# Expert gate and up products of a two-layer mixture-of-experts trunk with the weights stationary

## The chip, the cores and the metric

One core of one Trainium2 chip runs the whole program. The metric is the device time of one execution in microseconds (us); the kernel before takes 1674.31 us (median of 3 runs, 1674.31 to 1674.5). Everything is float32.

## What is computed

Two layers of a trunk over 768 tokens (512 latent tokens, 256 context tokens) of width 1024. A layer is: RMSNorm with a modulation computed from a condition vector, one input projection to 2400 columns, four kinds of attention, an output projection, a gated residual; then RMSNorm with modulation, a routed mixture of experts, a gated residual. The second layer needs the latent tokens only. The part that the change is named after:

```
def swiglu(x, wg, wu, wd):
    return (silu(x @ wg) * (x @ wu)) @ wd

out = swiglu(xs, ws_gate, ws_up, ws_down)              # shared expert, hidden width 256
for e in range(16):                                    # 16 experts, hidden width 256
    out = out + gates[:, e:e+1] * swiglu(xs, w_gate[e], w_up[e], w_down[e])
```

`gates` is zero but for two experts of each token: sigmoid scores of a router, the best of four groups of experts, the best two in it, weights normalised to sum 1. The output is the latent stream after a final RMSNorm.

## The kernel before

The order of work is written out by hand, engine by engine: five instruction lists (TensorE `pe`, VectorE `dve`, ScalarE `act`, GpSimd `pool`, SyncE `sp`) that meet at semaphores. SyncE issues nearly all loads and stores, in the order of its list; GpSimd issues the gathers and scatters.

**Start (layer 0).** SyncE loads the condition vectors and the identity (L577 to 580), four 2 MB pieces of the modulation weights (`mod_load`, L595), the bias and gain rows (`mod_rows`, L585, 588), two token tiles, panel 0 of the input projection, four more token tiles; then it waits for the first modulation product and loads panel 1, tables, small weights, and piece 4 of the modulation weights (L649 to 653). TensorE multiplies pieces 0 to 3 (`mod_product`, L1124); VectorE adds the bias rows (`mod_row`, L1830). TensorE turns each normalised token tile (L1142), ScalarE and VectorE write it modulated to `hT` (L885, L1820), and `unit` (L1211) multiplies it by the panel. ScalarE squares tile u+2 before it evacuates tile u+1; the semaphore of tiles 2 to 5 is one, for all four loads. Product 4 stands in the middle of unit 3, product 5 in the middle of unit 5, and so on.

**Experts.** Tokens are sorted by expert into blocks of 128 rows, each block of one expert. The program runs a fixed part and a loop over pairs of blocks whose number comes from the routing. In a block (`e_block`) TensorE does: gate product of block n (`e_in`, L1533), two transposes of block n-1's hidden rows (`hid_turn`, L1385), eight transposes of block n+1's tokens (`e_turn`, L1470), down product of block n-1 (`e_down`, L1543), up product of block n (`e_in` again). The gate and up products have the 128 tokens as the stationary side and the 256 columns of the weights as the moving side:

```
mm = pe.matmul((S0, S1)[b][:, 512 * w:512 * w + DE], XT[b][:, k, :], wgu[b][:, w, k * DE:(k + 1) * DE],
               start=k == 0, stop=k == KT - 1)
```

The result has tokens in its rows, so `hid` must be turned, and VectorE copies it to `hidT` (`e_hid_copy`, L2154) before the down product. VectorE also computes the sigmoid's sum, reciprocal and products (L2130 to L2149) and scales the output into `yb` (`e_out`, L2402). GpSimd scatters `yb` to `y_d` in memory at each token's two rows (L1733), and gathers the tokens of later blocks (L1721). SyncE loads 3 MB of weights a block (L773, L778).

**Seam and end.** The last two blocks of a layer (2 * pairs_2 + 2 and + 3) go partly another way: for the tiles below `late_tiles` (2 in layer 0, 4 in layer 1), `late_rows` (L1589) puts their rows in place by a matmul with a 0/1 matrix, and `c_late` (L2484) adds the result from PSUM. For the other tiles of layer 0 they are scattered (`late_scatter`, L1754). SyncE waits for the scatters, reads `y_d` by tile (L847), and VectorE adds (`y_add` L2442, `c_tile` L2473, L2474). In layer 1, GpSimd does both additions of tile 3 (L1776) and then the rstd steps of all four tiles (L1784, L1786), ScalarE squares (L1109), VectorE scales (`c_final`, L2491), SyncE stores (L857). At the seam SyncE also loads panel 1 of layer 1 (`win_load(1, 1)`), before it waits for the scatters.

**Routing of layer 1.** VectorE's list interleaves routing steps with the shared expert's. `route_places_hot` (L2283) writes the 0/1 matrix from which `route_table` (L1449) makes, by 8 matmuls, the table of tokens by block; `s_down` (L1434) is the shared expert's down product. GpSimd then copies an index (L1718) and gathers.

## Time and profile before

| | |
|---|---|
| Median of 3 runs | 1674.31 us |
| The profiled execution | 1669.1 us |
| its span, from first to last instruction | 1667.2 us |
| TensorE matmuls busy (PE) | 94% of the span |
| VectorE / ScalarE / GpSimd busy | 51% / 26% / 12% |
| TensorE in the chain that ended last | 84% |
| DMA moved | 284.77 MB, mean 171 GB/s |
| Mean granted TensorE clock | 0.987 of full speed |

PE is TensorE's matmuls, PEld its loads of the stationary side, which run beside them. Busy shares are means over stages with different limits; the chain of waits says which work ended last at each moment. In the rows below "issue" is time in which an engine waited for nothing that the profile shows, and a name such as SPq or DVEq is the sequencer of that engine.

### The profile page before, as it was taken

What the parts mean: (1) busy time and instruction counts of PE and PEld (TensorE: products, weight loads), DVE (VectorE), ACT (ScalarE), POOL (GpSimd) and SP (SyncE); (2) the same over time, 40 slices, a digit from 0 to 9 for tenths busy, and PEclk for the clock granted to TensorE, in tenths of its full rate; (3) what the DMA queues carried; (4) which work ended last, traced back from release to release, by engine and by line L of the source; (5) the groups of instructions that cost most, each with busy time, mean ns of one, the idle gap of its engine ahead of it and who ended that gap; (6) DMA issues with size and microseconds to landing.
All of it is one profiled execution on the core that took longest, in us unless ns stands there. A gap on an engine that the chain in (4) does not pass through costs nothing.

```text
span 1667.2 us, 24264 instructions
## 1 busy us (share of the span) xinstructions
PE 1574.3 (94%) x8994; PEld 1024.0 (61%) x8994; DVE 851.4 (51%) x1820; ACT 428.3 (26%) x922; POOL 200.6 (12%) x352
## 2 busy tenths in 40 slices
PE   3999999899999999999999799999899999999997
PEld 3655445666665567777777455555566666677774
DVE  1322433567666566455545621433667665644445
ACT  1312113455454410000000222113455541000001
POOL 0110202000000000212121110202000000022212
PEclk8999999999999999999999899999999999999999
DMA  9674321500001387589897673332401016478884
GB/s 337 197 279 150 104 31 20 190 1 35 18 26 39 105 300 283 171 330 335 326 336 275 228 261 116 137 82 36 174 1 39 14 51 230 181 262 307 321 319 185
DMA packets 107902, 284.77 MB, mean 171 GB/s; under 512 B 32544, under 2 KB 42206, under 8 KB 93406
## 3 DMA queue, kind: packets, MB, share of 16 engines
q1 hardware_dynamic: 97150, 262.48, 45.0%
q0 software_dynamic: 10656, 20.99, 3.4%
q8 instruction: 63, 1.03, 0.3%
q14 instruction: 33, 0.27, 0.1%
HBM read 265.47 MB, written 39.84 MB: 183 GB/s over the span
## 4 chain that ended last, share of the span: by engine, by line
PE 84%; DMA 5%; DVE 3%; SPq 3%; issue 2%; ACT 1%; POOL 0%; POOLq 0%; DVEq 0%; ACTq 0%
PE S L1211 16%; PE S L1533 13%; PE S L1279 9%; PE B L1344 7%; PE S L1543 6%; PE B L1327 6%; PE PT L1296 5%; PE B L1230 3%; PE B L1124 2%; DMA arena<-in_moe_w_up 2%; PE PT L1470 2%; PE S L1230 2%; PE PT L1434 1%; PE S L1410 1%; PE S L1417 1%
## 5 line engine op out<-in xcount | busy, mean ns | idle before, releaser
L1211 PE MATMUL S<-arena 128*128 128x512 f32 (+3 forms) x768 | 298.6, 539 | 6.4 <-issue 4.2
L1533 PE MATMUL S<-arena 128*128 128x256 f32 x1152 | 258.3, 381 | 4.7 <-DMA arena<-in_moe_w_up 3.6
L1533 PEld LDWEIGHTS S<-arena 128*128 128x128 f32 x1152 | 219.2, 191 | 51.5 <-issue 23.5
L1211 PEld LDWEIGHTS S<-arena 128*128 128x128 f32 x768 | 141.2, 192 | 127.7 <-issue 109.3
L989 ACT ACTIVATE arena<-S,nmax 128x768 f32<-128x768 f32 (+1 forms) x200 | 161.8, 812 | 164.6 <-DVE nmax L2016 123.2
L2016 DVE TENSOR_REDUCE nmax<-S 128x1 f32<-128x768 f32 (+1 forms) x168 | 133.1, 825 | 77.8 <-PE S L1279 77.5
L1279 PE MATMUL S<-arena 64*128 64x256 f32 (+5 forms) x720 | 161.7, 499 | 5.8 <-ACT arena L989 4.0
L1344 PE MATMUL B<-arena 128*128 128x512 f32 x320 | 156.5, 613 | 1.9 <-DVE arena L2070 1.9
L1296 PEld LDWEIGHTS PT<-cst,arena 128*128 128x128 f32 x832 | 94.6, 141 | 84.1 <-issue 56.9
L1296 PE MATMUL PT<-cst,arena 128*128 128x128 f32 x832 | 121.2, 278 | 18.8 <-issue 11.3
L1543 PE MATMUL S<-arena 128*128 128x512 f32 x288 | 130.1, 594 | 1.2 <-DVE arena L2154 1.2
L1279 PEld LDWEIGHTS S<-arena 64*128 64x128 f32 (+2 forms) x720 | 75.1, 187 | 68.2 <-issue 59.0
L1008 ACT ACTIVATE arena<-PT 128x768 f32<-128x768 f32 (+3 forms) x100 | 81.1, 811 | 118.5 <-PE PT L1299 59.5
L1327 PE MATMUL B<-arena 128*64 128x128 f32 x1664 | 108.5, 277 | 2.5 <-issue 2.4
L1327 PEld LDWEIGHTS B<-arena 128*64 128x64 f32 x1664 | 89.4, 137 | 22.5 <-issue 22.5
L1041 ACT ACTIVATE arena<-S 128x256 f32<-128x256 f32 x36 | 13.8, 383 | 346.0 <-PE S L1533 346.0
L1344 PEld LDWEIGHTS B<-arena 128*128 128x128 f32 x320 | 54.4, 189 | 53.1 <-issue 48.8
L1543 PEld LDWEIGHTS S<-arena 128*128 128x128 f32 x288 | 52.4, 192 | 55.0 <-issue 55.0
L2131 DVE RECIPROCAL arena<-arena 128x256 f32<-128x256 f32 x46 | 80.6, 1753 | 1.6
L1124 PE MATMUL B<-arena,cs 128*32 128x128 f32 x1536 | 51.3, 291 | 28.7 <-DMA arena<-in_w_mod 17.1
L1830 DVE TENSOR_TENSOR arena<-B,arena 128x128 f32<-128x128 f32 x24 | 6.9, 290 | 137.0 <-PE B L1124 112.1
L2154 DVE COPY arena<-B 128x256 f32<-128x256 f32 x36 | 15.3, 424 | 114.0 <-PE B L1385 114.0
(306 smaller groups left out, 1789.1 us busy)
## 6 DMA issues: line engine op xcount, KB each, us to landing
arena<-in_w_mod SPq DMA_DIRECT2D x24, 2048.0 KB, 10.6
arena<-in_moe_w_gate SPq DMA_DIRECT2D x36, 1024.0 KB, 6.0
arena<-in_moe_w_up SPq DMA_DIRECT2D x36, 1024.0 KB, 8.9
arena<-in_moe_w_down SPq DMA_DIRECT2D x36, 1024.0 KB, 6.0
arena<-in_w_in SPq DMA_DIRECT2D x6, 2048.0 KB, 11.4
arena<-y SPq DMA_DIRECT2D x20, 512.0 KB, 7.0
arena<-mod SPq DMA_DIRECT2D x16, 512.0 KB, 15.9
arena<-in_tokens SPq DMA_DIRECT2D x12, 512.0 KB, 9.5
```

Of the source, the lines that this page charges most:

```text
L989: act.activation(p_buffer(k, m)[:, 0:nk], (S0, S1)[m][:, 0:nk], ACT.Exp, bias=nmax[:, 2 * k + m:2 * k + m + 1], accum_out=rsum[:, 2 * k + ...
L1008: act.activation(t_buffer(k, 1)[:, 0:width], PT[:, 0:width], ACT.Copy).then_inc(s["pt_s"], 1)
L1124: mm = pe.matmul(bank[32 * q:32 * q + 32, 0:MODQ], cs[:, k, :], mod_w[l][n][:, k, q * MODQ:(q + 1) * MODQ], start=k == 0, stop=k == KT - 1)
L1211: mm = pe.matmul(ubank[u % 4][:, c0:PANEL_W[p]], hT[:, k, t * P:(t + 1) * P], panel[p][:, k, c0:], start=k == 0, stop=k == KT - 1)
L1230: mm = pe.matmul(nb_bank(n)[:, 0:c1 - c0], panel[4][:, k, w0:w0 + P], hT[:, k, c0:c1], start=k == 0, stop=k == KT - 1)
L1279: mm = pe.matmul((S0, S1)[m][:, c0:c1], qk[rows, qs, cols], qk[rows, ks, NTOK - nk + c0:NTOK - nk + c1], start=True, stop=True)
L1296: tr = pe.transpose(PT[:, c0:c0 + P], p_buffer(k, m)[:, c0:c0 + P], ident)
L1327: mm = pe.matmul(B6[64 * m:64 * m + 64, 0:P], vals[:, (NTOK - nk) // P + j, v0 + 64 * m:v0 + 64 * m + 64], bufs[m][:, j * P:j * P + P], st ...
L1344: mm = pe.matmul(B7[:, :], OT[t % 2][:, j, :], wout[:, j, c * 512:(c + 1) * 512], start=at_ == 0, stop=at_ == KT - 1)
L1533: mm = pe.matmul((S0, S1)[b][:, 512 * w:512 * w + DE], XT[b][:, k, :], wgu[b][:, w, k * DE:(k + 1) * DE], start=k == 0, stop=k == KT - 1)
L1543: mm = pe.matmul((S0, S1)[b][:, c * 512:(c + 1) * 512], hidT[b][:, k, :], wdn[b][:, k, c * 512:(c + 1) * 512], start=k == 0, stop=k == 1)
L2016: dve.tensor_reduce(nmax[:, 2 * k + m:2 * k + m + 1], Sm[:, 0:nk], AX.X, ALU.max, negate=True).then_inc(s["neg_max"], 1)
```

## The change

- Gate and up products: the weights are the stationary side (two pieces of 128 of the 256 hidden columns), the 128 turned tokens the moving side. The result has hidden columns in its rows. The turn, its copy and `hidT`'s use in experts go; the down product reads `hid`, and `down_load` arranges the weights' rows as (k p) instead of (p k).
- First loads: the condition vectors, the identity and layer 0's bias and gain rows are issued by ScalarE. SyncE issues piece 4 of the modulation weights before panel 1. VectorE normalises tile 0 after the modulation rows and tile 1 after tile 0's evacuation.
- Seam: `win_load(1, 1)` is issued after the reads of tiles 0 and 1. `c_tile` is split in `c_first` and `c_second`, and VectorE evacuates tile t before the first.
- Layer 1: `route_places_hot` before the last up multiplication; `route_table` before the last turn of hidden rows; the first gathers take their index from `token_of` directly; the first down loads wait for gather 0.
- End of layer 1: rows of tiles 2 and 3 in block 2 * pairs_2 + 2 are scattered, and their reads wait for that; `late_rows` of those tiles is left only for the last block. `c_late(2)` and `c_late(3)` move forward by one step.

```diff
         for n in range(4):
             mod_load(0, n, 0)
-        sp.wait_ge(zeros_set, 2)
-        mod_rows(0, 0, NMCH, (0, 1))
         for t in range(2):
             x_load(t)
         win_load(0, 0)
         for t in range(2, T):
             x_load(t)
-        sp.wait_ge(s["mod_mm"], 1)
+        mod_load(0, 4, 2)
         win_load(0, 1)
         sp.dma_start(cst[:, first:], cst_d[:, first:]).then_inc(tables_in, 16)
         gain_load(0)
         small_load(0)
-        mod_load(0, 4, 2)
         sp.wait_ge(zeros_set, 3)
         for layer in range(DEPTH):
             sp.dma_start(relpad[1:61, layer * P + 48:layer * P + 79], A["na_rel_bias"][layer].rearrange("h a b -> (h a) b")).then_inc(rel_step, 16)
...
     def down_load(b, e):
-        src = A["moe_w_down"][l].rearrange("e (p k) n -> e p (k n)", k=2)[bass.ds(e, 1)].rearrange("o p n -> (o p) n")
-        sp.dma_start(wdn[b].rearrange("p a b -> p (a b)"), src).then_inc(s[f"e_dn_in{b}"], 16)
+        src = A["moe_w_down"][l].rearrange("e (k p) n -> e p k n", k=2)[bass.ds(e, 1)].rearrange("o p k n -> (o p) k n")
+        sp.dma_start(wdn[b], src).then_inc(s[f"e_dn_in{b}"], 16)
     def expert_of(blk):
...
         in_load(0, 0, e0)
         in_load(1, 1, e1)
-        sp.wait_ge(s["e_idx"], ge(0) + 2)
+        sp.wait_ge(e_x_in[l][0], 16)
         down_load(0, e0)
         down_load(1, e1)
         sp.dma_start(fgain, A["final_norm"].partition_broadcast(P)).then_inc(s["c_x_in"], 16)
...
         for b in range(2):
             w_load(2 * i + 2 + b, b)
-    if l == 0:
-        win_load(1, 1)
     for b in range(2):
         sp.wait_ge(e_stored[l][b], 16 * (pairs_1 + 1))
...
     for t in range(nt):
         if t == late_tiles[l]:
+            if l == 0:
+                win_load(1, 1)
             for b in range(2):
                 sp.wait_ge(e_stored[l][b], 16 * (pairs_1 + 2))
                 sp.sem_inc(s["spare_seen"], 1)
+        if l and t == LATE_FIRST:
+            sp.wait_ge(e_stored[l][0], 16 * (pairs_1 + 2))
+            sp.sem_inc(s["spare_seen"], 1)
         if l == 0 and t == T - 1:
             sp.wait_ge(late_y, late_tiles[0])
...
 @block.scalar
 def _(act):
+act.dma_start(csrc[:, 0, :], A["c"].rearrange("a (p k) -> (a p) k", k=KT)).then_inc(cond_in, 16)
+act.dma_start(csrc[:, 1, :], A["c_ctx"].rearrange("(p k) -> p k", k=KT)).then_inc(cond_in, 16)
+first = at["ident"][1]
+act.dma_start(cst[:, 0:first], cst_d[:, 0:first]).then_inc(consts_in, 16)
 act.wait_ge(cond_in, 32)
 act.activation(ctmp[:, :, :], csrc[:, :, :], ACT.Exp, scale=-1.0).then_inc(s["small_exp"], 1)
+act.wait_ge(zeros_set, 2)
+for r in range(2):
+    act.dma_start(mod_row0[r:P:32], A["b_mod"][0].rearrange("(n q c) -> q n c", q=4, c=MODQ)).then_inc(s["mod_rows_in"], 16)
+    for half in range(2):
+        gain = A[("norm_mix", "norm_ffn")[half]][0]
+        act.dma_start(mod_norm_at(0, half)[r:P:32], gain.rearrange("(n q c) -> q n c", q=4, c=MODQ)).then_inc(s["mod_rows_in"], 16)
 for l in range(DEPTH):
     g = lambda t: t + T * l
...
         s_down(1)
         s_turn_hid(2)
         s_up(3)
+        pe.wait_ge(s["r_took"], 2)
+        route_table()
         pe.wait_ge(s["s_hts"], g(2) + 1)
         s_turn_hid(3)
-        pe.wait_ge(s["r_took"], 2)
-        route_table()
         s_down(2)
         s_down(3)
...
     def e_in(blk, b, w):
-        for k in range(KT):
-            mm = pe.matmul((S0, S1)[b][:, 512 * w:512 * w + DE], XT[b][:, k, :], wgu[b][:, w, k * DE:(k + 1) * DE],
-                           start=k == 0, stop=k == KT - 1)
+        for h in range(2):
+            to = (S0, S1)[b][:, 512 * w + h * P:512 * w + (h + 1) * P]
+            for k in range(KT):
+                mm = pe.matmul(to, wgu[b][:, w, k * DE + h * P:k * DE + (h + 1) * P], XT[b][:, k, :], start=k == 0, stop=k == KT - 1)
         mm.then_inc(s[("e_g", "e_u")[w]], 1)
     def e_down(blk, u, b):
         pe.wait_ge(s[f"e_dn_in{b}"], 16 * (u + 1 + NBK[0] // 2 * l))
-        pe.wait_ge(s["e_htv"], ge(blk) + 1)
+        pe.wait_ge(s["e_hid"], ge(blk) + 1)
         for c in range(2):
             for k in range(2):
-                mm = pe.matmul((S0, S1)[b][:, c * 512:(c + 1) * 512], hidT[b][:, k, :], wdn[b][:, k, c * 512:(c + 1) * 512],
+                mm = pe.matmul((S0, S1)[b][:, c * 512:(c + 1) * 512], hid[b][:, k * P:(k + 1) * P], wdn[b][:, k, c * 512:(c + 1) * 512],
                                start=k == 0, stop=k == 1)
         mm.then_inc(s["e_d"], 1)
...
         pe.wait_ge(s["e_t_s"], ge(blk) + 1)
         e_in(blk, b, 0)
         last = not first or b
-        if last:
-            hid_turn("e_", ge(blk) - 1, hid[1 - b])
         if more:
             e_turn(blk + 1, u + b, 1 - b, False)
         if last:
...
     late_rows(0, 1, [0, 1])
     late_rows(1, 0, [1])
     late_rows(1, 1, [0, 1])
-    for t in range(2, late_tiles[l]):
-        late_rows(t, 0, [0, 1])
+    for t in range(LATE_FIRST, late_tiles[l]):
         late_rows(t, 1, [0, 1])
     if l == 0:
         pe.wait_ge(s["e_d"], 2 * pairs_1 + 2)
-        spare_pairs(pe, l, pairs, [("e_tr", 2), ("e_g", 2), ("e_u", 2), ("e_ht", 2), ("e_d", 2)])
+        spare_pairs(pe, l, pairs, [("e_tr", 2), ("e_g", 2), ("e_u", 2), ("e_d", 2)])
 @block.gpsimd
...
                                 out_offset=bass.IndirectOffsetOnAxis(ap=idx2[n], axis=0)).then_inc(e_stored[l][b], 16)
     pool.wait_ge(s["s_tr"], gend)
+    def first_gather(b):
+        if l:
+            pool.wait_ge(s["e_tr"], ge(b) - 1)
+        pool.sem_inc(s["e_idx"], 1)
+        pool.indirect_dma_start(out=xg[b], out_offset=None, in_=h2_d[l], bounds_check=nt * P - 1, oob_is_err=False,
+                                in_offset=bass.IndirectOffsetOnAxis(ap=token_of[:, b:b + 1], axis=0)).then_inc(e_x_in[l][b], 16)
     for b in range(2):
-        e_gather(b, b, l == 0)
+        first_gather(b)
     for b in range(2):
-        e_gather(2 + b, b, False)
+        e_gather(2 + b, b)
     def late_zeros(b):
...
             rstd_of(1, t)
         spare_pairs(pool, l, pairs, [("e_idx", 2), ("e_row_idx", 2)])
     else:
+        late_scatter(2 * pairs_2 + 2, 0)
         pool.wait_ge(s[f"c_y_in{TL - 1}"], 16 * TOPK * (l + 1))
         for j in range(TOPK):
             pool.tensor_tensor(x3[TL - 1], x3[TL - 1], y12[l][TL - 1][:, j, :], ALU.add).then_inc(pool_y, 1)
...
         dve.tensor_copy(modcol.rearrange("p r w k -> p w k r"), src).then_inc(s["modcol_set"], 1)
     if l == 0:
-        for n in range(2):
-            mod_row(0, n, (B6, B7)[n])
-        for t in range(2):
-            normalise(0, t)
-        for n in range(2, 4):
+        for n in range(4):
             mod_row(0, n, (B6, B7)[n % 2])
         mod_gain(0, 0)
+        normalise(0, 0)
         modcol_of(0, S0)
         evac_hT(0, 0)
+        normalise(0, 1)
     def rope(ch, x, t, rot, heads, outs):
...
         s_gate_mul(3)
         route_slots()
         route_blocks_hot()
+        route_places_hot()
         s_up_mul(3)
-        route_places_hot()
         s_out(0)
         route_rows()
         pairs, pairs_1, pairs_2 = pair_counts(dve, l)
...
     e_out(2 * pairs_2 + 3, pairs_2 + 1, 1, False, y_adds)
     R_START[0] += ch.n
-    def c_tile(t):
-        ch = Count(dve, s["v_c"], TOPK * 2 + t - 2)
+    def c_first(t):
         dve.wait_ge(s[f"c_y_in{t}"], 16 * TOPK * (l + 1))
-        ch.done(dve.tensor_tensor(x3[t], x3[t], y12[l][t][:, 0, :], ALU.add)).sync()
+        dve.tensor_tensor(x3[t], x3[t], y12[l][t][:, 0, :], ALU.add).then_inc(s["v_c"], 1)
+    def c_second(t):
+        dve.wait_ge(s["v_c"], TOPK * 2 + t - 1)
         dve.tensor_tensor(x3[t], x3[t], y12[l][t][:, 1, :], ALU.add).then_inc(s["c_x3"], 1)
     def c_late(t):
...
         c_late(1)
         normalise(1, 0)
         for t in range(nt):
+            evac_hT(1, t)
             if t + 2 < nt:
-                c_tile(t + 2)
-            evac_hT(1, t)
+                c_first(t + 2)
             if t + 1 < nt:
                 normalise(1, t + 1)
+            if t + 2 < nt:
+                c_second(t + 2)
         dve.wait_ge(s["e_y"], 2 * pairs_1 + 2)
-        spare_pairs(dve, l, pairs, [("e_t_v", 2), ("v_e", 6), ("e_hid", 2), ("e_htv", 2), ("e_y", 2)])
+        spare_pairs(dve, l, pairs, [("e_t_v", 2), ("v_e", 6), ("e_hid", 2), ("e_y", 2)])
     else:
         y_add(2, 0)
         c_late(0)
         y_add(2, 1)
         c_late(1)
+        c_late(2)
         c_final(0, 0)
-        c_late(2)
+        c_late(3)
         c_final(1, 1)
-        c_late(3)
         c_final(2, 0)
         c_final(3, 1)
```

Left out: names of semaphores, the four VectorE instructions that split the row indices of block 2 * pairs_2 + 2 at tile `LATE_FIRST` = 2, and the same calls' changed arguments.

## Rows read from the trace of the kernel before

**Rows 1.** The page: chain that ended last, and costliest groups (busy us, mean ns).

```profile
PE 84%; DMA 5%; DVE 3%; SPq 3%; issue 2%; ACT 1%; POOL 0%; POOLq 0%; DVEq 0%; ACTq 0%
...
L1533 PE MATMUL S<-arena 128*128 128x256 f32 x1152 | 258.3, 381 | 4.7 <-DMA arena<-in_moe_w_up 3.6
```

**Rows 2.** Chain of waits, expert blocks: start us, duration us, what, instructions.

```profile
771.49 6.91 PE S L1533 x32
778.39 0.23 PE B L1385 x2
778.62 0.90 PE PT L1470 x8
779.52 3.44 PE S L1543 x8
```

**Rows 3.** Chain of waits, 128x128 stationary sides, then L1327's 128x64.

```profile
663.33 2.60 PE B L1449 x24
...
368.10 0.66 PE PT L1296 x6
...
370.35 1.46 PE B L1327 x24
```

**Rows 4.** Timeline of the start: start, duration, engine, what [idle before <-releaser].

```profile
2.12 11.15 SPq L595 DMA_DIRECT2D arena<-in_w_mod  x4
...
29.00 0.49 DVE L1830 TENSOR_TENSOR arena<-B,arena 128x128 f32<-128x128 f32 x2 [24.86 <-DMA arena<-in_norm_ffn]
...
40.47 1.06 ACT L879 ACTIVATE arena<-arena 128x1024 bf16<-128x1024 f32 x1 [1.57 <-DMA arena<-in_tokens]
...
63.09 3.07 PE L1124 MATMUL B<-arena,cs 128*32 128x128 f32 x64 [3.67 <-DMA arena<-in_w_mod]
```

**Rows 5.** Chain of waits, start, fifth modulation product and after.

```profile
48.69 14.27 DMA arena<-in_w_mod
...
66.17 5.44 PE S L1211 x16
...
72.48 4.74 PE S L1211 x16
77.22 1.88 PE B L1124 x64
```

**Rows 6.** Chain of waits, seam between the layers.

```profile
906.08 8.03 DMA y<-arena
...
920.99 0.70 PE B L1385 x2
...
923.40 3.75 PE S L1543 x8
...
937.95 2.60 issue
940.55 4.50 PE S L1211 x8
```

**Rows 7.** Chain of waits, head of layer 1.

```profile
1436.85 3.47 PE S L1417 x16
...
1440.84 1.14 DVE arena L2283
...
1442.18 3.08 PE B L1449 x16
1445.25 5.73 PE PT L1434 x8
```

**Rows 8.** Windows, head of layer 1: busy by engine, PEclk, DMA share, GB/s.

```profile
1444.00:1446.00 2.00, 2.00 (x7) 1.56 (x8) 0.55 (x3) 0.00 (x0) 0.00 (x0) 0.50 1.04 438
```

**Rows 9.** Chain of waits, end of layer 1.

```profile
1627.08 6.08 DMA y<-arena
...
1660.91 1.28 DVE arena L2491
```

**Rows 10.** Timeline, end of layer 1, GpSimd's additions.

```profile
1646.79 5.91 POOL L1776 TENSOR_TENSOR arena<-arena 128x1024 f32<-128x1024 f32 x2 [18.73 <-DMA arena<-y]
```

29 lines of the change are left out of this document (12 added, 17 removed).

## Prediction

> **What bounds the kernel now.** I read the page's chain of waits first: TensorE (PE) holds 84% of it, so whatever neither shortens TensorE's list nor removes a wait of TensorE is worth nothing [rows 1]. Then the chain stretch by stretch, to see what TensorE waits for where it is not busy.
> - Expert blocks (36 of them: 1152 gate/up matmul instructions at 32 each [rows 1]). 
> - Seam between the layers and head of layer 1: chains over several engines, with TensorE idle and then at the lower clock [rows 6 to 8].
> - Tail: TensorE's late rows, then a short chain of VectorE, ScalarE and GpSimd [rows 9, 10].
>
> **The change part by part** (the sum is made against the profiled execution: 1669.1 us, of which 1667.2 is the span).
>
> *Gate and up turned.* Each product becomes 2 x 8 matmuls of 128 columns: 64 instructions a block in place of 32. What a 128-column instruction with a 128x128 stationary side costs no ordinary matmul of the trace shows. From below: 24 instructions of 28 columns take 2.60 us, 108 ns each; their streams are short, so this is the pace of the weight loads [rows 3]. Same shapes: six transposes of contiguous data take 0.66 us, 109 to 110 ns, and eight of strided data 0.90 us, 112 ns [rows 2, 3]. From above: the value products, 128 columns with stationary sides of 64 columns, two beside each other in the array, take 1.46 us for 24, or 122 ns a pair [rows 3]. Both operands of the new product are contiguous and the weight loads are not the slower side, so I take 109.5: 64 x 109.5 = 7.01 us, +0.10 a block. Against it stand 0.23 us for the turn. So 36 x 0.10 - 34 x 0.23 = -4.2 us (the last turn of each layer lies in the next parts). At 112 it would be +1.5, at 108 -7.8, at 122 +24. Nothing else holds TensorE in a block: its down product needs the hidden block, which VectorE finishes more than 4 us earlier, while the next gate product and the token transposes run. The loop goes at 11.4 us in place of 11.5, and three blocks wait for an up weight already; each shortened period is waited for there, and the down weights come in pieces of half the length. I charge +0.4 us. Blocks: **-3.8 us** (-8 to +3).
>
> The Trainium skill ("TensorE: Matmul & The Clock Gate", LDWEIGHTS and Back-to-back issue gap) gives a load of 128 columns 107 ns, which the 108 ns above bear out, but says that in a stream the spacing is set by both operations together and lies about 1.45 times above the gap without loads at 128 columns; that rule speaks against this change and is the second rival below.
>
> *First loads.* Three small loads leave SyncE's (SP) queue, so the 2 MB modulation loads start at 0.73 in place of 2.12 us: 1.4 us earlier [rows 4]. From there the DMA engines are full, so everything up to the last tokens shifts by those 1.4 us. The bias rows now go through ScalarE's queue. At present VectorE waits for them until 29.00 and TensorE's third and fourth modulation products with it [rows 4]; that wait goes, and the first tile could start some 4.5 us earlier. But it is late next that counts: ScalarE squares tile 2 ahead of evacuating tile 1, and VectorE normalises tile 2 ahead of its part of tile 1; both need the four last token loads, which land at 40.47 now [rows 4] and at 39.1 then. So the second tile starts 1.4 us earlier, not 4.5. If the bias rows still landed behind the weights, this would be about the same 1.4.
>
> A second rule sits beside this: the Trainium skill ("DMA: Bandwidth & Descriptors", Queues, rings and completion order) has each DMA engine take turns between queue rows packet by packet, so the bias rows should land within a few us rather than behind 8 MB. With it or without it the sum is the same.
>
> Modulation load 4 moves ahead of panel 1, the tables and a dozen small loads. It is issued at 48.69 and TensorE starts on it at 63.09 after 3.67 us idle [rows 4, 5]; the product then takes 3.07 us where the next one takes 1.88, and the sixteen matmul instructions behind it 5.44, where the next sixteen take 4.74 [rows 5]. With the load in by about 46 us all three go: 3.67 + 1.2 + 0.7 = 5.6 us. Next late is load 5, which still waits for product 4 to free its slot: it gets the 11.05 us from 66.17 to 77.22 less the clock's 0.7, in which it lands without a wait today. VectorE's reordering hides behind the token loads. Start: **-7.0 us** (-4 to -10).
>
> *Seam.* Panel 1's load (2 MB) is issued behind the y rows rather than in front of the scatter. The scatter lands after 8.03 us; the same step of layer 1, without such a load, takes 6.08 [rows 6, 9]. With some 0.3 us that SP then spends on the second buffer's scatter, the last up product is multiplied 2.3 us earlier. Behind it now come turn, late rows, copy, down product: 2.41 us from the turn's start to the down product's [rows 6]. The late rows' matmuls run in the idle time instead and the down product starts at once: -2.4, and it takes 3.44 instead of 3.75 (-0.3). Then VectorE sums tile 2 ahead of its part of tile 0's evacuation: ScalarE's part is done at 937.95, and the first unit waits 2.60 us more [rows 6]. With the evacuation first nearly all of that goes: -2.5. The two halves of the sum that follow fit beside 5.6 us of TensorE a tile. The first eight instructions take 4.50 us where eight take 2.37 (half of 4.74, [rows 5]); TensorE fell to the lower clock in the wait that is now shorter. I count half of those 2.1. Seam: **-8.5 us** (-7 to -10).
>
> *Head of layer 1.* Routing places go before the last up multiplication: VectorE starts them when it is idle at 1439.7, not at 1440.84 [rows 7]. The table product starts at about 1441.1 rather than 1442.18, and is not delayed by the turn. In the gaps before it TensorE fell from 2.4 to 1.2 GHz (granted clock 0.50, [rows 8]): the table's 16 instructions took 3.08 us and the next eight 5.73, against 1.73 (16 x 108) and 3.44 [rows 2, 3, 7]. A gap of 0.8 us in place of the gaps that summed to 1.4 should not bring that: 1.1 + 1.35 + 2.3 = 4.7, less 0.5 us that the last down product then waits for VectorE, and the turn that moves behind (0.2). The gather without its index copy is about 3 us earlier and stays off the path; down weights now wait for it, with over 8 us in hand. Head: **-4.0 us** (0 to -5).
>
> *Tail.* Eight instructions of late rows go (3.44 us like the down product's eight, [rows 2]) and the down product starts 1.4 us earlier, but tiles 2 and 3 can be read only when a scatter of block n-1 has landed. That scatter starts at about 1636.9 and lands by its like (6.08 us, somewhat less at half the rows, [rows 9]) at 1642 to 1643; four reads follow, tile 3 in at about 1650, where all eight were in by 1646.79 [rows 10]. GpSimd's two additions (5.91 us) start then and stand in its queue ahead of all four rstd steps, so the first output can be scaled only near 1656.8. The last output is scaled by 1663.2, now by 1662.2 [rows 9]: the wait for TensorE is exchanged for one for GpSimd. Tail: **+1.0 us** (-1.5 to +4).
>
> Sum: -3.8 - 7.0 - 8.5 - 4.0 + 1.0 = **-22.3 us**: 1646.8 by the profiled execution. The median of the runs, 1674.31, lies 5.2 above that execution; I apply the same difference: **1652**.
>
> **Rivals.**
> - *The clock stays low* at the seam and at layer 1's head. For: TensorE still idles in both. Against: the gaps are shorter than those in which it fell. Price 1.0 + 3.6: 1657.
> - *Loads and streams overlap only in part at 128 columns.* Where each load must wait for part of the stream before it, the pace is the pair's 122 ns: 36 x 64 x 12.5 ns = +29 us, in the gate and up products, all on TensorE; the change is slower from 119 ns on. For: the value products [rows 3]. Against: transposes of the same shape keep 109 to 112 [rows 2, 3]. Time 1681, slower. Taken at the page's factor 1.45 the pace would be 158 ns and the time some 110 us higher, which the transposes exclude.
> - *The turn buys nothing*: at 112 ns, the strided transposes' pace, the blocks stay at 11.5 us (+5.7 us against the forecast), and all gain comes from the edges: 1658. For: same shapes. Against: the new operands are contiguous, as those that keep 109.5 [rows 3].
> - *The tail costs more*: the scatter lands 3 us later, behind the reads of tiles 0 and 1, and with it all behind: 1655. For: the first scatter of the seam was held up by a load in just this way [rows 6]. Against: at the tail the reads ahead of it are in by 1641.
>
> **How the numbers follow.** Forecast 0.60 (own range 1646 to 1657), low clock 0.10, turn buys nothing 0.13, costly tail 0.09, partial overlap 0.07, rest 0.01. Bounds all one way reach 1642 and 1668; the range 1642 to 1665 leaves the partial overlap and little else outside. Under 0.2% (3.3 us) the measurement tells nothing. Faster: all but the partial overlap and mixtures of the bad ends, 0.92; same 0.02; slower 0.06.
>
> **What would show it.** Gate/up pieces of 64 instructions in 7.0 us, and a block in 11.3; a block of 11.6 or more refutes the pace. No wait before the fifth modulation product, the second tile's unit at 43.3. Scatter at the seam in 6 us, no turn, first unit of layer 1 some 10 us after the last down product ends. Clock 1.00 through the table product. At the end GpSimd's additions start near 1650 minus what was gained before, and TensorE is done well before them. The forecast fails if the 128-column pace exceeds 112 ns or a stretch that I hold for covered (panel 1, load 5, the gather) shows TensorE waiting for a DMA.

## The result, and the profile after

The changed kernel takes 1655.7 us (median, 1654.9 to 1657.5) against 1674.3 us before: the runs compared give 0.9901 of the time, 95% interval 0.9884 to 0.9918 (the two medians alone give 0.989). Its profiled execution took 1654.9 us (span 1653.0), 14.2 us less than the profiled one of before. The forecast was 1652, the range 1642 to 1665. The median came out 3.7 us from the forecast, but partly by luck. Between the profiled executions, against which the sum was made, 22.3 us were forecast and 14.2 measured; 4.4 of the 8.1 that are missing come back because the profile of before lay 5.2 us below its median and that of after only 0.8. Nor did the parts come out: the turned products, 3.8 us of the sum in the blocks and 2.4 at the seam, are worth 0.6 us a layer in the blocks (V3 below) and let the seam's down product start 0.9 sooner (E1).

The seven stretches below add up to the span; cuts are starts of TensorE matmuls, from each profile's timeline. *Blocks* reach from the start of a layer's first gate product to the start of its last up product, *seam* from there to the first unit of layer 1, *head* from the last shared up product to the first expert product, *tail* from the last up product of layer 1 to the end. (Where the expectations below say "from the last gate product of layer 0", their 4.43 us are counted from this last up product.) "Waits" are TensorE's waits for up weights in layer 0's blocks.

```
kernel                       start  blocks0  waits(n)  seam  layer 1  head   blocks1  tail   span
before                       682.7  230.35   3.0 (2)  27.50  496.13  19.59  179.25  31.68  1667.2
after                        680.0  229.77   4.1 (6)  18.87  497.31  16.04  178.53  32.48  1653.0
E1 turned undone             679.8  226.58   1.3 (2)  19.77  496.92  17.16  179.86  34.81  1654.9
E2 turned alone              684.7  237.80   7.7 (4)  27.53  496.57  19.62  178.53  30.75  1675.5
E3 96 columns                680.8  230.83   5.5 (5)  19.09  496.98  17.10  178.71  34.39  1657.9
E4 strided                   681.5  233.58   1.6 (1)  19.05  497.15  17.16  183.65  31.91  1664.0
E5 routing order undone      680.9  231.49   5.8 (5)  19.30  496.78  17.06  178.85  32.62  1657.0
E6 panel load first          681.4  233.36   6.3 (5)  25.59  496.17  16.05  179.62  32.51  1664.7
E7 modulation load 4 late    680.2  232.10   5.3 (4)  19.51  496.13  17.08  178.84  33.94  1657.8
V1 combined                  677.3  236.94   8.0 (6)  18.87  496.80  17.17  179.05  30.67  1656.8
after, once more             681.9  231.63   5.5 (5)  19.58  496.28  16.05  179.28  31.68  1656.4
E8 layout alone              679.1  228.60   2.8 (3)  20.35  495.58  17.15  180.68  32.44  1653.9
V2 separate waits            676.5  224.24   0        19.68  495.88  16.04  177.53  32.73  1642.6
V3 as V2, turned undone      678.1  224.80   0        20.24  496.29  17.09  178.15  32.13  1646.8
```

One profile of a kernel differs from the next by some 2 us in a stretch where a transfer or the clock decides (compare the two rows of after), and all runs of before beside the experiments lie between 1663.7 and 1677.7 us. So single experiments are read by their stretch and by their chains, not by their total. V1, V2 and V3 share three further edits, described at V1.

The blocks, from the chain of waits (start us, us, what); it answers to [rows 2]:

```profile
735.27 7.14 PE S L1543 x64
742.42 0.89 PE PT L1478 x8
743.31 3.44 PE S L1552 x8
746.74 7.14 PE S L1543 x64
```

64 instructions in 7.14 us are 111.6 ns each. Turn (0.23) and copy are gone, the product is 0.23 longer, and the period is 11.47 us, as before. The page's row of the product (busy, mean ns of one | idle before it, and what ended it) shows what else matters there: TensorE waits for up weights (before: 3.6 us over both layers, [rows 1]).

```profile
L1543 PE MATMUL S<-arena 128*128 128x128 f32 x2304 | 265.6, 275 | 5.9 <-DMA arena<-in_moe_w_up 4.9
```

The start, from the timelines of VectorE and of TensorE (L1219 is a unit, L1132 a modulation product, L1834 VectorE's part of the evacuation), against [rows 4, 5]:

```profile
15.11 0.29 DVE L1844 TENSOR_TENSOR arena<-B,arena 128x128 f32<-128x128 f32 x1 [9.07 <-DMA arena<-in_norm_ffn]
```

```profile
43.95 4.01 PE L1219 MATMUL S<-arena 128*128 128x352 f32 x8 [2.47 <-DVE arena L1834]
...
60.26 1.96 PE L1132 MATMUL B<-arena,cs 128*32 128x128 f32 x64
62.15 5.00 PE L1219 MATMUL S<-arena 128*128 128x352 f32 x16
...
74.57 5.64 PE L1219 MATMUL S<-arena 128*128 128x352 f32 x15
```

The bias rows are in by 15.11 (29.00 before), and the fifth modulation product does not wait. But the second unit does, 2.47 us, and runs its first eight instructions at a lower clock: 4.01 us where eight take 2.37. The fifth unit starts 3.95 us earlier than before, the seventh 4.46.

The seam, first the timeline of the queues, then the chain, against [rows 6]:

```profile
903.32 0.98 POOL L1738 DMA_INDIRECT y<-arena  x1 [0.86 <-POOL arena L1730]
907.25 1.76 SPq L845 DMA_DIRECT2D arena<-y  x4
909.05 2.32 SPq L610 DMA_DIRECT2D arena<-in_w_in  x2
```

```profile
909.94 3.57 PE S L1543 x32
913.51 0.86 PE PT L1596 x2
914.37 3.43 PE S L1552 x8
...
925.89 1.11 PE PT L1150 x8
927.44 1.16 ACT arena L893 x3
928.60 0.04 issue
928.64 4.33 PE S L1219 x8
```

From GpSimd's scatter to the y reads pass 3.93 us (8.45 before, of which the transfer 8.03). VectorE adds the y rows in front of the last hidden product; they are there in time now, and the down product follows the last up product at once. The wait before the first unit is gone too: 0.04 us of "issue" where before had 2.60. The first eight instructions of the unit are still at the lower clock (4.33 us, 4.50 before). Head and tail, again by the chain, against [rows 7, 9]:

```profile
1429.01 1.24 DVE arena L2291
...
1430.44 1.94 PE B L1457 x16
1432.38 0.31 PE B L1393 x2
1432.68 3.44 PE PT L1442 x8
...
1441.99 3.81 PE S L1543 x32
...
1623.15 3.60 DMA y<-arena
...
1628.16 6.91 DMA arena<-y
1635.15 2.37 POOL arena L1790
...
1646.55 1.28 DVE arena L2503
```

Table product (L1457) and down product (L1442) run at full clock here: 1.94 us and 3.44, where before had 3.08 and 5.73. The tail has lost TensorE from its chain, and has GpSimd and two transfers in its place.

### The profile page after: what moved, and what is told of

Same layout as the page of the kernel before. It is cut to its first block, busy times and chain, and to the rows that moved or that the text cites. A ratio compares the mean times of both kernels' runs of the same rounds, so it can differ in the third digit from the quotient of the medians.

```text
span 1653.0 us, 26346 instructions
## 1 busy us (share of the span) xinstructions
PE 1569.8 (95%) x10066; PEld 1052.5 (64%) x10066; DVE 836.3 (51%) x1788; ACT 428.8 (26%) x922; POOL 197.9 (12%) x349
## 4 chain that ended last, share of the span: by engine, by line
PE 82%; DMA 7%; DVE 4%; SPq 2%; issue 2%; ACT 1%; POOL 0%; POOLq 0%; DVEq 0%; ACTq 0%
PE S L1219 15%; PE S L1543 13%; PE S L1287 9%; PE B L1352 8%; PE S L1552 6%; PE B L1335 6%; PE PT L1304 6%; DMA arena<-in_moe_w_up 3%; PE B L1238 3%; PE B L1132 2%; DMA arena<-in_w_mod 2%; PE PT L1478 2%; PE S L1238 2%; PE S L1418 1%; PE PT L1442 1%
## 5 line engine op out<-in xcount | busy, mean ns | idle before, releaser
L1219 PE MATMUL S<-arena 128*128 128x512 f32 (+3 forms) x768 | 299.4, 540 | 6.3 <-ACT arena L893 3.8
L1543 PEld LDWEIGHTS S<-arena 128*128 128x128 f32 x2304 | 263.7, 192 | 23.9 <-issue 23.9
L1543 PE MATMUL S<-arena 128*128 128x128 f32 x2304 | 265.6, 275 | 5.9 <-DMA arena<-in_moe_w_up 4.9
L1219 PEld LDWEIGHTS S<-arena 128*128 128x128 f32 x768 | 141.2, 192 | 127.7 <-issue 107.5
L1287 PE MATMUL S<-arena 64*128 64x256 f32 (+5 forms) x720 | 163.5, 504 | 4.7 <-ACT arena L997 2.9
L1304 PEld LDWEIGHTS PT<-cst,arena 128*128 128x128 f32 x832 | 94.7, 141 | 84.1 <-issue 56.9
L1304 PE MATMUL PT<-cst,arena 128*128 128x128 f32 x832 | 121.3, 278 | 18.8 <-issue 11.3
L1287 PEld LDWEIGHTS S<-arena 64*128 64x128 f32 (+2 forms) x720 | 75.7, 189 | 67.7 <-issue 59.5
L2175 DVE COPY arena<-PT 128x512 f32<-128x512 f32 x36 | 24.9, 691 | 138.8 <-PE PT L1478 138.8
L1552 PEld LDWEIGHTS S<-arena 128*128 128x128 f32 x288 | 52.1, 191 | 52.7 <-issue 52.7
L1132 PE MATMUL B<-arena,cs 128*32 128x128 f32 x1536 | 52.6, 295 | 20.0 <-DMA arena<-in_w_mod 18.7
## 6 DMA issues: line engine op xcount, KB each, us to landing
arena<-in_w_in SPq DMA_DIRECT2D x6, 2048.0 KB, 11.3
```

The costliest lines, as they stand in the source:

```text
L1132: mm = pe.matmul(bank[32 * q:32 * q + 32, 0:MODQ], cs[:, k, :], mod_w[l][n][:, k, q * MODQ:(q + 1) * MODQ], start=k == 0, stop=k == KT - 1)
L1219: mm = pe.matmul(ubank[u % 4][:, c0:PANEL_W[p]], hT[:, k, t * P:(t + 1) * P], panel[p][:, k, c0:], start=k == 0, stop=k == KT - 1)
L1287: mm = pe.matmul((S0, S1)[m][:, c0:c1], qk[rows, qs, cols], qk[rows, ks, NTOK - nk + c0:NTOK - nk + c1], start=True, stop=True)
L1304: tr = pe.transpose(PT[:, c0:c0 + P], p_buffer(k, m)[:, c0:c0 + P], ident)
L1543: mm = pe.matmul(to, wgu[b][:, w, k * DE + h * P:k * DE + (h + 1) * P], XT[b][:, k, :], start=k == 0, stop=k == KT - 1)
L1552: mm = pe.matmul((S0, S1)[b][:, c * 512:(c + 1) * 512], hid[b][:, k * P:(k + 1) * P], wdn[b][:, k, c * 512:(c + 1) * 512], start=k == 0, s ...
```

## Experiments

**E1, the turned products alone undone** in the changed kernel, and **E2, they alone** in the kernel before. The diff is E1's; E2 makes the reverse edit in the kernel before.

```diff
-for h in range(2): for k in range(KT):
-    pe.matmul(S[.. h*P ..], wgu[.. k*DE + h*P : k*DE + (h+1)*P], XT[b][:, k, :], ...)
+for k in range(KT): pe.matmul(S[.. DE ..], XT[b][:, k, :], wgu[.. k*DE:(k+1)*DE], ...)
+hid_turn(...); e_hid_copy(...)       # and down weights "(p k)": one piece of 8 KB a partition
```

> The changed kernel with the turned products alone undone: tokens stationary again, the hidden block turned and copied, down weights in one piece of 8 KB a partition; start, seam, routing and tail orders stay. Theory A (in the blocks 64 instructions at 111.6 ns against 32 at 216 ns cost +0.23 us, which the turn's 0.23 us pay back): blocks stay at 11.47 us, and the only loss is turn and copy in front of the down product at the seam, +1 to +2 us, and 0 to +0.5 at the tail: 1656 to 1658 by the profiled execution (the changed kernel's is 1654.9). Rival B (the products gave the 3.8 us that were forecast and something else took them): +6 us, 1661. Rival C (the short pieces of the down weights let the scatters land 2 us earlier at both layers' ends): scatter to y read back at about 6 us in place of 3.9, +3 to +5 in all, 1658 to 1660.

> The kernel before with the turned products alone (with the down weights' layout that they need). Theory A: blocks at 11.47 us as before; gain only where turn and copy stood in front of the last down product: 2.4 us at the seam, 1.4 at the end of layer 1 and 0.2 at the head of layer 1: 1665 to 1667 by the profiled execution (before: 1669.1). Rival B (pace under 110 ns): another 3.8 us, 1661 to 1663. Rival C (pieces of 4 KB): the first scatter of the seam lands in about 6 us in place of 8.03, and the last of layer 1 in 4 in place of 6.1.

E1: 1657.5 us (1656.8 to 1658.0), 0.9913 (0.989 to 0.9937) of before; E2: 1671.1 us, 0.999 (0.9976 to 1.0005). By E2's interval the turned products by themselves can't be told from no change, and the 1665 to 1667 expected of its profiled execution were missed: it took 1677.7, 6.6 us above the median of its runs, in long waits for up weights. In E1 the seam's down product comes 0.9 us later (5.33 us from the start of the last up product, not 4.44), as theory A had it; its tail is 2.3 us longer, where 0 to 0.5 was expected. In E2 the seam is 27.53, before 27.50, and its chain says where the gain went:

```profile
931.43 5.24 PE S L1544 x8
...
944.76 1.95 PE PT L1142 x8
...
948.31 1.72 issue
```

The down product starts 8.93 us from the start of the last up product, before 10.14, so 1.2 us are gained; but it takes 5.24 us where before has 3.75, and the transposes 1.95 for 1.10: the lower clock (0.74 granted from 932 to 937 us) takes 2.3 us back, and a shorter wait before the unit (1.72 for 2.60) gives 0.9. Rival B falls with E1, whose blocks were faster, not slower. TensorE's waits in its layer 0 blocks (us in total, times, longest):

```profile
PE S L1541 <- DMA arena<-in_moe_w_up: 1.3, 2, 1.0
```

Rival C falls for the seam: with pieces of 8 KB the y reads follow the scatter in 3.44 us (899.09 to 902.53) in E1, and with pieces of 4 KB in 8.05 us in E2, where the panel load stands in front. At the end of layer 1 E2 did what C said (3.4 us from scatter to y reads, before 6.2), but over all fourteen profiles this step takes 3.4 to 6.5 us with 4 KB and 3.4 to 6.3 with 8 KB, so it doesn't follow the pieces.

**E3, 96 of 128 moving columns** (the last 32 tokens of a block are left out of the gate and up products); **E4, a strided stationary side.**

```diff
-pe.matmul(to[.. 128 columns], wgu[.. k*DE + h*P : k*DE + (h+1)*P], XT[b][:, k, :], ...)
+pe.matmul(to[.. 96 columns],  wgu[.. k*DE + h*P : k*DE + (h+1)*P], XT[b][:, k, 0:96], ...)   # E3
+pe.matmul(to[.. 128 columns], wgu[.. k*DE + h : (k+1)*DE : 2], XT[b][:, k, :], ...)          # E4, down weights "(p k)"
```

> The changed kernel with the gate and up products over 96 of the 128 tokens of a block (the last 32 tokens' hidden values are left out), everything else as it is: the stream of a matmul instruction is a quarter shorter, the 128x128 weight load unchanged. Theory A (the 111.6 ns are the pace of the weight loads): pieces of 64 instructions at 108 to 112 ns, 6.9 to 7.14 us, block 11.2 to 11.47 us. Rival D (they are the stream's): 84 ns, 5.4 us, block 9.7 us where the loads allow it; over 36 blocks up to -60 us. Rival E (the 11.47 us are set by the weight transfers and not by TensorE): the block stays at 11.47 with TensorE waiting for w_gate, w_up or w_down.

> The changed kernel with the down weights as before (one piece of 8 KB a partition) and the stationary side of the gate and up products taken with every second column, so that the hidden values come out in the order which that layout needs. Theory A (the pace does not hang on the stride): pieces of 64 at 7.14 us, blocks at 11.47. Rival F (a strided stationary side costs the 112 against 109 ns that the transposes showed): 7.3 us or more, block 11.6, +5 us. Of the layout: rival C has the scatter at the ends of both layers land in about 6 us again, with 3 waits for up weights in place of 7; without it the scatter stays at 3.9 us and only the waits may change. By A without C 1655, by A with C 1657 to 1659.

E3 takes 1659.9 us in its one run. Its chain in the blocks:

```profile
736.65 7.12 PE S L1543 x64
743.77 0.91 PE PT L1478 x8
```

A quarter less to stream, and 7.12 us in place of 7.14: the 111.6 ns are not the pace of the stream (D falls), and TensorE is busy without a gap there (E falls for these blocks). That it is the pace of the weight loads shows in E4, which changes only the stationary side of these products. E4 is 1666.1 us, 0.9964 (0.9941 to 0.9986); its chain:

```profile
736.51 7.53 PE S L1543 x64
...
748.37 7.53 PE S L1543 x64
```

117.7 ns an instruction: the same load costs 6 ns more when it reads every second column. Rival F is right (it had 7.3 us or more, and a block of 11.6): blocks of 11.86 us, busy 278.5 us in all against 265.6. The scatter of the seam starts at 908.24 and the y reads at 911.53 with pieces of 8 KB, so C falls again.

**E5, the routing order undone**: places of the rows behind the last shared up multiplication, fourth turn ahead of the table product.

```diff
-route_places_hot(); s_up_mul(3)                 # VectorE
+s_up_mul(3); route_places_hot()
-wait r_took; route_table(); s_turn_hid(3)       # TensorE
+s_turn_hid(3); wait r_took; route_table()
```

> The changed kernel with the routing order alone undone: VectorE multiplies the last up product of the shared experts before it places the rows, and TensorE turns the fourth hidden block before the table product; the first gathers stay without their index copies. Theory A (the order closes the gap in which TensorE's clock fell): the table product starts about 1 us later and takes 3.1 us in place of 1.94, the eight down instructions behind it about 5.7 in place of 3.44; from the first unit of layer 1 to the first expert product 516.5 us in place of 513.4: +3 us, 1658 by the profiled execution. Rival (the gain came from the gathers without index copy): these 513.4 us stay, +0 to +0.5.

1659.1 us (1653.4 to 1663.5). The head is 17.06 us against 16.04. Its chain:

```profile
1428.63 3.47 PE S L1425 x16
...
1432.63 1.14 DVE arena L2291
...
1433.96 1.94 PE B L1457 x16
1435.90 3.52 PE PT L1442 x8
```

The table product starts 5.33 us behind the start of the up product, as before (5.33, [rows 7]), with 1.85 us of it without a product, but at full clock. Theory A is half right: the order gives 1.0 us; whether the clock falls in the same gap changes from execution to execution. In the table above the old order has it in two of three profiles (19.59, 19.62; 17.06 without), the new order has a shorter one in seven of eleven (17.08 to 17.17 us; 16.04 to 16.05 without).

**E6, panel 1's load back in front of the last scatters; E7, modulation load 4 back behind panel 1 and the small loads.**

```diff
+if l == 0: win_load(1, 1)                       # E6
 for b in range(2): sp.wait_ge(e_stored[l][b], 16 * (pairs_1 + 1)) ...
-mod_load(0, 4, 2)                               # E7
 win_load(0, 1); ...; small_load(0)
+mod_load(0, 4, 2)
```

> The changed kernel with panel 1's load of layer 1 back in front of the wait for the last scatters. Theory A (the load holds the scatter up): scatter to y reads 8 us in place of 3.9, and from the last gate product of layer 0 to its last down product 6.5 to 8.5 us in place of 4.43: +2 to +4 us, 1657 to 1659. Rival (the turn and copy and the late rows in front of the down product were what took the 10.34 us; the scatter is hidden): scatter 8 us, but the 4.43 us stay, +0 to +0.5. Where TensorE then waits longer, the units behind start at a lower clock: +0.5.

> The changed kernel with modulation load 4 back behind panel 1, tables and small loads. Theory A (the load's place was worth the 4 us that the start gained up to the seventh unit): the fifth product starts 2 to 3.7 us later than at 60.26 with a wait for its weights, takes about 3 us in place of 1.96, and the seventh unit starts at 78 to 79 in place of 74.57: +4 us, 1659. Rival (the gain came from the first loads on ScalarE's queue): seventh unit at 75 to 76, +0.5 to +1. Of the clock loss at the start of attention (1.36 us, in the changed kernel alone): if it hangs on how early TensorE gets there, it is smaller or gone here.

E6: 1666.9 us, 0.9963 (0.9944 to 0.9983). Its chain at the seam:

```profile
908.30 8.07 DMA y<-arena
916.47 0.34 SPq L845
916.85 4.85 DMA arena<-y
...
922.86 0.43 DVE arena L2161
923.42 5.37 PE S L1552 x8
...
936.88 1.83 PE PT L1150 x8
...
940.31 0.04 issue
```

Theory A is right and its price too low. The load holds the scatter for 4.2 us; VectorE's addition waits for the y rows and stands in its queue ahead of the hidden product, so TensorE's down product is 4.2 us late (8.66 us from the start of the last up product, not 4.44); and after that wait the clock is down: 5.37 us for 3.43, transposes 1.83 for 1.11. Together the seam is 25.59 us in place of 18.87. What E6 keeps is the order of VectorE's evacuation, and with it the wait before the unit stays away, late scatter or not (0.04 us; before 2.60, E2 1.72).

E7: 1658.9 us (1656.6 to 1664.1). TensorE's timeline:

```profile
61.83 1.95 PE L1133 MATMUL B<-arena,cs 128*32 128x128 f32 x64 [1.50 <-DMA arena<-in_w_mod]
63.71 5.00 PE L1220 MATMUL S<-arena 128*128 128x352 f32 x16
...
76.14 4.35 PE L1220 MATMUL S<-arena 128*128 128x352 f32 x12
```

A wait of 1.50 us, no fall of the clock, and the seventh unit at 76.14 in place of 74.57: the load's place was worth 1.6 us, between theory A (4) and the rival (0.5 to 1). The other 2.9 of 4.46 came with the first loads and VectorE's new order there. E7 has no fall of the clock at the start of attention; of the ten profiles up to V1 only it and before are without one, which is too little to put it down to load 4.

**V1, a combined version.** Three edits: separate semaphores for the tokens of tiles 2 to 5, late modulation rows of layer 1 ahead of the token stores, the tail's order as before.

```diff
-X_IN = ["x_in0", "x_in1"] + ["x_rest_in"] * (T - 2)
+X_IN = [f"x_in{t}" for t in range(T)]
 mod_load(1, 4, 0)
+mod_rows(1, LATE, NMCH, (1,))
 sp.wait_ge(s["c_x3"], T)
-late_scatter(2 * pairs_2 + 2, 0)                # layer 1; and TensorE's late rows of tiles 2 and 3 back
```

> The changed kernel with three edits in three separate stretches. (1) Each of tiles 2 to 5 of the first tokens has its own semaphore, so squares of tile 2 no longer wait for tile 5: the second unit starts without the 2.47 us idle of TensorE and without the lower clock behind it (4.01 us for eight instructions in place of 2.37, transposes 1.37 in place of 0.9); seventh unit at 70.5 to 72.5 in place of 74.57. Rival: the mod load is late next, and the seventh unit gains under 1 us. (2) The four row loads of layer 1's late modulation are issued ahead of the wait for the last token sum: modulation load 5 of layer 1 is issued 2.4 us earlier, and the 1.2 us wait of the product at 972.20 goes (-1.2; rival: the load is slowed by the token stores, 0). (3) The tail order of layer 1 as before the change, with the turned products kept: last gate product to end 30.8 us in place of 32.3 (-1.5; rival: TensorE's late rows are back in front of the last sums and nothing is gained, 0 to +1). Sum -5 (-1 to -7): 1650 by the profiled execution.

1653.6 us (1649.9 to 1658.7), 0.9895 (0.9869 to 0.9921). Its edits did about what they should in their stretches: start 677.3 in place of 680.0, tail 30.67 in place of 32.48, no wait for modulation load 5 of layer 1 (0.8 us in after; the second profile of after has none either, so this edit's worth isn't shown). But the profiled execution took 1658.7 us, where 1650 was expected, and all of the excess is in the layer 0 blocks:

```profile
PE S L1539 <- DMA arena<-in_moe_w_up: 8.0, 6, 2.5
```

The waits cost more than their own length: these blocks are 12.7 us longer than V2's below, which have no such wait, and the granted clock was 0.96 from 760 to 800 us and from 840 to 880, and 1.00 from 800 to 840.

**E8, the layout of the down weights alone; V2, separate waits for gate and up weights; V3, V2 with the turned products undone; and after once more.** The gate product waits on a semaphore that both loads count up, so TensorE waits for up weights that it needs only 8 us later. E8 is E1 with the down weights left in two pieces of 4 KB a partition. V2 is V1 with the edit below (tiles 3 to 5 then share a semaphore again); V3 is V2 with the turned products undone and down weights in one piece of 8 KB.

```diff
-sp.dma_start(wgu[b][:, n, :], src).then_inc(s[f"e_gu_in{b}"], 16)
+sp.dma_start(wgu[b][:, n, :], src).then_inc(s[f"e_{('gu', 'up')[n]}_in{b}"], 16)
-pe.wait_ge(s[f"e_gu_in{b}"], 32 * (u + 1 + NBK[0] // 2 * l))
+pe.wait_ge(s[f"e_gu_in{b}"], 16 * (u + 1 + NBK[0] // 2 * l))
 ...
+pe.wait_ge(s[f"e_up_in{b}"], 16 * (u + 1 + NBK[0] // 2 * l))
 e_in(blk, b, 1)
```

> The changed kernel once more, unaltered, as the measure for the two kernels beside it: 1655 to 1658. By theory A its layer 0 blocks wait 3 to 6 us for up weights, whatever the rest does.

> The kernel with the turned products undone (tokens stationary, hidden block turned and copied), but with the down weights in two pieces of 4 KB a partition, as the changed kernel has them; the turn takes contiguous halves of the hidden block. TensorE's work of a block is the same as with one piece of 8 KB. Theory A (the shorter pieces make every weight load land later: medians 6.4, 9.6 and 7.0 us against 5.8, 8.9 and 6.6, and the first product of a block waits for the later of gate and up): waits for up weights in layer 0 of 4 to 8 us, as in all six profiles with 4 KB pieces and contiguous weights so far, in place of 1.3; layer 0's blocks 229 to 233 us in place of 226.6; 1660. Rival (the waits come from the turned products or from chance): 1 to 3 us, blocks 226 to 228, 1657.

> The combined version with one more edit: gate and up weights of a block have semaphores of their own, so the gate product waits for the gate weights alone and the up product for the up weights, which is 8 us later (token tiles 2 to 5 then have two semaphores, not four). Theory A (TensorE waits in the blocks only for up weights that it does not need yet): no wait for up weights in layer 0 (8.0 us in the combined version), its blocks at 225 to 226.5 us, 1643 to 1648 by the median. Rival G (the transfers bound the blocks, 0.9 of the DMA engines' time is busy: the wait only moves to the gate weights or the up product): blocks stay at 229 us or more, 1650 to 1653.

> The version with separate waits for gate and up weights (1647.6 us), with the turned products undone and the down weights in one piece of 8 KB: the worth of the turned products where no weight load holds TensorE. Theory A (in a block the product's +0.23 us and the turn's -0.23 us cancel; a gain is left only in front of the last down product of each layer): layer 0's blocks at 224.2 us as with them (223.5 to 225), from the last gate product of layer 0 to its last down product 5.3 us in place of 4.43, the last stretch of layer 1 longer by 0.5 to 2.3: +1 to +3 us, 1649 to 1651. Rival B (the turned products gain the 4 us of the forecast once the weights are there): layer 0's blocks at 226 us or more, 1652 to 1654. Rival H (they cost more than they bring): 1645 to 1647.

After once more: 1658.4 us (1654.6 to 1669.2), 0.9929 (0.9905 to 0.9954), with 5.5 us of waits, as expected. E8: 1654.9 us (1653.5 to 1660.0), 0.9904 (0.9881 to 0.9926), so undoing the turned products costs nothing here either. Its waits of 2.8 us are in the rival's range, its blocks of 228.6 between the two, and its time is below both (1660 and 1657). Its gate and up loads land later than E1's in layer 0's blocks (median 6.3 and 9.5 us from issue to landing, E1 5.8 and 8.9). But V3, with pieces of 8 KB, has 6.3 and 9.5 as well, and E4 6.2 and 9.3, so a price of the short pieces isn't shown. The eight profiles with turned products, a contiguous stationary side and the joint wait have 4.1 to 8.0 us of waits, the three without turned products 1.3 to 3.0; whether the products, the pieces or chance make the difference stays open.

V2: **1647.6 us** (1644.5 to 1648.5), 0.9856 (0.9841 to 0.9871), 10.8 us below after on the same chip. V1's edits are in it, so the separate waits are not worth all of that: V1's median is 6.0 us above V2's (on another chip; 0.9895 and 0.9856 of before), and layer 0's blocks are 5.5 and 7.4 us longer in the two profiles of after. No wait is left in layer 0's blocks, 224.24 us, and rival G falls: the transfers keep up, only the joint wait was late. Its chain:

```profile
741.17 7.14 PE S L1539 x64
...
752.64 7.14 PE S L1539 x64
```

V3: 1648.3 us (1647.5 to 1649.5), 0.9853 (0.983 to 0.9876): level with V2. Where no load disturbs, layer 0's blocks are 224.80 with the turn and 224.24 without it, layer 1's 178.15 and 177.53; theory A holds, B is excluded, and H (1645 to 1647) isn't met. The 0.6 us a layer are one wait: in the last block, which has no token transposes behind the turn, TensorE waits for VectorE's copy:

```profile
PE S L1548 <- DVE arena L2167: 0.6, 1, 0.6
```

Of the +1 to +3 expected in all 0.7 came: the seam is 0.6 longer (the down product 0.9 later, as in E1), the tail 0.6 shorter.

## Why the prediction was right in sum and wrong in parts

The sum came out by luck in part. Against the profiled execution 8.1 of 22.3 us are missing: 4.3 at the start, 2.5 in the blocks, 1.2 in layer 1, 0.5 in the head, less 0.3 at seam and tail together. The step from profile to median then gave 4.4 back. (The bounds all one way add up to 1640 and 1670, not to the 1642 and 1668 of the prediction.)

- **Blocks, -3.8 forecast, -1.3 measured (230.35 to 229.77 and 179.25 to 178.53).** The term that failed is the pace: 109.5 ns from six contiguous transposes; it is 111.6, so 64 take 7.14 us and the period is 11.47, where 7.0 and 11.3 were to show it. This is the rival "the turn buys nothing", at 0.13. I took contiguity and shape for the whole of the cost. E3 shows that the stream doesn't set the pace, E4 that the stationary side does, by its stride too. The mean of one load is 192 ns for the contiguous product L1543 and for the strided token transposes L1478, and 141 for the contiguous transposes L1304: the product's load went with the dearer kind, and why isn't shown. V3 against V2 is the direct answer: in the blocks turned products are worth 0.6 us a layer. That is the wait for VectorE's copy in the last block, which the sum had at nothing. The Trainium skill ("TensorE: Matmul & The Clock Gate", LDWEIGHTS) reckons a load by its columns alone, 107 ns for 128; E4's 117.7 against 111.6 at equal columns shows that here the layout counts as well. The factor of 1.45 that the prediction took from its section Back-to-back issue gap, the rule that spoke against the change, gave 158 ns, and this product doesn't come near: 111.6 is 1.04 times 107. (The skill has the factor over the gap without loads, which no run here shows; the prediction put it on the transposes' 109.)
- **What held blocks back was in plain sight**, and I charged it +0.4: the waits for up weights. In layer 0 with the joint wait they took 1.3 to 8.0 us from profile to profile, and more with the clock behind them. Separate waits shorten layer 0's blocks by 1.8 us (V3 against E1) to 12.7 (V2 against V1), the turned products by 0.6 (V2 against V3). The prediction called them "a wait for an up weight" and did not ask whether the waiting product needs up weights. It does not.
- **Start, -7.0 forecast, -4.5 at the seventh unit, -2.7 at the first expert product.** Load 4's stall was priced at 5.6 us; E7 gives 1.6, since in E7 the late load lands 1.3 us sooner than in before and TensorE comes to it 0.9 us later: 1.50 us of wait for 3.67, and no fall of the clock behind it (1.95 us for 3.07). First loads and VectorE's order gave 2.9 rather than 1.4. Tokens as the limit of the second unit was right (43.95 us, forecast 43.3); its new price was not foreseen: 2.5 us idle and 1.6 of lower clock. With other semaphores for the tokens the seventh unit of V1 and V2 starts at 71.82 and 72.04, 2.8 and 2.5 us earlier. Another 1.4 us went at the start of attention in a gap in which the clock fell (2.91 us for eight instructions of L1287, 1.54 in E7), and did not in before.

The windows (us, busy of PE, PEld, DVE, ACT, POOL; then granted clock, DMA share, GB/s) of after, then of E7, show the stretch:

```profile
308.00:311.00 3.00, 3.00 (x12) 1.32 (x14) 0.81 (x3) 0.87 (x1) 0.00 (x0) 0.50 1.04 415
```

```profile
308.00:311.00 3.00, 2.71 (x21) 1.77 (x23) 1.90 (x6) 1.29 (x3) 0.00 (x0) 1.00 1.01 350
```

- **Seam, -8.5 forecast, -8.6 measured, for other reasons.** The panel load was priced at 2.3 us; E6 gives 6.7, because everything behind the scatter waits and the clock falls with it. Turn and copy were priced at 2.4; without the late scatter they are worth 0.9 up to the down product (E1, V3), and in E2, with it, 1.2, which the clock took back. Two errors cancelled. For all other edits of the seam 1.9 us are left (27.50 to 25.59 in E6), turned products among them. The evacuation's order was priced at 2.5: its wait of 2.60 us did go, in after and in E6 alike, but no run undoes that order alone.
- **Layer 1 between seam and head, nothing forecast, +1.2 measured** (496.13 to 497.31): 0.8 is a wait of TensorE for modulation load 5, issued behind the token stores. The second profile of after has 496.28 and no such wait, so this is no fixed cost; the other 0.4 stays open.
- **Head, -4.0 forecast, -3.55 measured.** The order is worth 1.0 (E5; 1.1 forecast); 2.5 are a fall of the clock that before and E2 had and E5 had not. That the new order keeps the clock up isn't shown: with it the head had a smaller fall in seven of eleven profiles. That after had none was luck.
- **Tail, +1.0 forecast, +0.8 measured.** The exchange of TensorE for GpSimd happened as described, with the first addition at 1635.15. With turned products the old order takes 30.75 and 30.67 us in two profiles and 32.73 in a third, whose last y read took 10.5 us; the new one 31.7 to 34.4 in seven. By these profiles it costs rather than gains; the ranges overlap.

## What to carry to other kernels

When the operands of a small matmul change places, count the weight loads and take their pace from a product and not from the cheapest transpose; here the two transposes saved (0.23 us) were worth no more than the 32 loads added. Before pricing a loop, look at each wait and ask which instruction first needs what it waits for: two loads on one semaphore cost 1.8 to 12.7 us in layer 0's blocks here, and the change of products brought 0.6. And put a large load behind, not in front of, a small transfer that others wait for: its price here was the delay (4.2 us) plus what the clock took from TensorE afterwards (2.5).

## What the hardware showed that was not expected

- The load of a 128x128 fp32 stationary side paces matmuls of 96 and of 128 columns alike (111.3 and 111.6 ns an instruction, E3 and after); at a stride of two elements it is 117.7 ns (E4).
- The clock's falls in short gaps are not the same from execution to execution (granted clock 0.50 or 1.00): with the same 1.85 us ahead of the table product the head took 19.6 us twice and 17.06 once.
- Small rows sent through ScalarE's queue landed by 15.1 us beside 8 MB of weights in SP's; sent behind the weights in SP's own queue they kept VectorE waiting until 29.0. The Trainium skill ("DMA: Bandwidth & Descriptors", Queues, rings and completion order) has the engines take turns between queues; the trace agrees.
